# A two-layer decoder trunk on one core: a head's transposes behind the next query product, the first expert tiles' rows gathered in the router's block, blocks that end without GpSimd's drain

## What is computed

```python
for l in range(DEPTH):                       # 2 layers, 1024 tokens, D_MODEL = 1024
    h = rmsnorm(x, norm_mix[l])
    x = x + (hybrid_mixer(h, ...) if l % 2 == 0 else swa_mixer(h, ...))
    x = x + cross_attention(rmsnorm(x, norm_xattn[l]), mem_k, mem_v, w_q[l], w_o[l])
    x = x + hier_moe(rmsnorm(x, norm_ffn[l]), ...)
return rmsnorm(x, final_norm)

# hybrid_mixer, part B (4 heads; q and k are two maps of 64 each, v is 128 wide)
a = softmax(q0 @ k0.T) - lam * softmax(q1 @ k1.T)       # causal
o = rmsnorm(a @ v, subln_g) * (1 - lambda_init)         # a head's output, then the output projection
# hier_moe: 1 of 4 groups, top 2 of its 8 experts; tokens sorted by expert
xs = t[tok_sorted]; gu = ragged_dot(xs, w_gate_up, group_sizes)
y = ragged_dot(silu(gu[:, :512]) * gu[:, 512:], w_down, group_sizes) * weight
```

## Time and profile before

| | before |
|---|---|
| median of 3 runs | 2696.58 us (2696.14 to 2696.95) |
| the profiled execution's own time | 2695.93 us |
| its span | 2694.1 us |
| TensorE busy | 2460.8 us (91%) |
| VectorE, ScalarE, GpSimd busy | 858.0, 411.2, 286.7 us |
| hybrid block | 66 to 525 us |
| routers' blocks | 734 to 832 us, 1977 to 2075 us |
| experts' blocks | 833 to 1439 us, 2076 to 2649 us |

### The profile page before, as it was taken

The page is one execution under the profiler, slowest core; times in us unless marked ns, Lnnn a source line. Parts: engine busy times, 40 slices in busy tenths (PEclk is TensorE's granted clock), DMA queues, the critical chain, the costliest instruction groups (busy, mean ns, idle before and its releaser), DMA issues. The chain is left out here.

```text
span 2694.1 us, 28504 instructions
## 1 busy us (share of the span) xinstructions
PE 2460.8 (91%) x10112; PEld 1320.8 (49%) x10112; DVE 858.0 (32%) x1509; ACT 411.2 (15%) x1012; POOL 286.7 (11%) x303
## 2 busy tenths in 40 slices
PE   6999999999995999999996989989995999999992
PEld 4667676645642444444444754634552444444440
DVE  3244352653243111111114472765235111111114
ACT  2122121201210000000001150501220000000001
POOL 0000000230000000000003040341000000000003
PEclk9999999999997999999998999999997999999996
DMA  6010101105136999999996100210024899999996
GB/s 211 24 32 16 39 18 67 39 0 230 62 145 225 387 403 402 402 403 405 403 402 198 43 15 25 71 39 32 1 89 176 313 402 402 402 403 403 404 397 234
DMA packets 204306, 563.21 MB, mean 209 GB/s; under 512 B 33104, under 2 KB 70864, under 8 KB 204112
## 3 DMA queue, kind: packets, MB, share of 16 engines
q1 hardware_dynamic: 182208, 493.64, 48.3%
q0 software_dynamic: 12000, 42.74, 4.6%
q10 hardware_dynamic: 10032, 25.96, 2.5%
HBM read 506.19 MB, written 55.05 MB: 208 GB/s over the span
## 5 line engine op out<-in xcount | busy, mean ns | idle before, releaser
L2020 PE MATMUL pair<-W,yT 128*128 128x512 f32 x1056 | 465.7, 599 | 0.0
L2020 PEld LDWEIGHTS pair<-W,yT 128*128 128x128 f32 x1056 | 199.4, 191 | 241.4 <-issue 239.0
L2033 PE MATMUL pO<-hT,yT 128*64 128x512 f32 x1056 | 233.9, 595 | 12.8 <-ACT yT L2126 11.8
L2062 PE MATMUL pair<-W,yT 128*128 128x512 f32 x528 | 232.3, 593 | 0.0
L834 PE MATMUL pU<-hT,W 128*128 128x256 f32 x768 | 174.7, 380 | 5.2 <-DVE W L976 2.4
L2167 DVE TENSOR_TENSOR tmp<-probT,pair 128x512 f32<-128x512 f32 x33 | 22.7, 688 | 460.4 <-ACT probT L2105 460.4
L834 PEld LDWEIGHTS pU<-hT,W 128*128 128x128 f32 x768 | 142.2, 190 | 26.2 <-issue 5.0
L2062 PEld LDWEIGHTS pair<-W,yT 128*128 128x128 f32 x528 | 97.7, 190 | 112.1 <-issue 112.1
L2033 PEld LDWEIGHTS pO<-hT,yT 128*64 128x64 f32 x1056 | 75.4, 137 | 150.1 <-issue 150.1
L2171 DVE TENSOR_TENSOR tmp<-probT,pO 64x512 f32<-64x512 f32 x33 | 22.4, 679 | 358.8 <-ACT probT L2109 358.8
L2074 PE MATMUL pO<-yT 128*64 128x512 f32 x528 | 120.6, 598 | 1.6 <-DVE yT L2175 1.6
(11 more groups left out here) (330 smaller groups left out, 3079.0 us busy)
## 6 DMA issues: line engine op xcount, KB each, us to landing
W<-in_moe_w_gate_up_dram SPq DMA_DIRECT2D x132, 1024.0 KB, 13.1
hT<-in_moe_w_gate_up_dram SPq DMA_DIRECT2D x132, 1024.0 KB, 16.5
W<-in_moe_w_down_dram SPq DMA_DIRECT2D x66, 1024.0 KB, 16.1
yT<-in_moe_w_down_dram SPq DMA_DIRECT2D x66, 1024.0 KB, 13.6
y_rows<-prob ACTq DMA_DIRECT2D x33, 512.0 KB, 6.7
y_rows<-qk SPq DMA_DIRECT2D x31, 512.0 KB, 6.1
W<-in_hyb_w_in_dram SPq DMA_DIRECT2D x24, 512.0 KB, 3.7
y_rows<-yT ACTq DMA_DIRECT2D x66, 128.0 KB, 6.4
```

The source lines that it names most:

```text
L2020: ins = nc.tensor.matmul(A[:, 512 * h:512 * h + 512], xt_l[:, k, :], gu_l[:, k, 512 * h:512 * h + 512], start=(k == 0), stop=(k == KD - 1))
L2033: ins = nc.tensor.matmul(pO[HS * (1 - h):HS * (1 - h) + HS, :], xt_s[:, k, :], gu_s[:, k, 512 * h:512 * h + 512], start=(k == 0), stop=(k ...
L2062: ins = nc.tensor.matmul(B[:, 512 * h:512 * h + 512], ht_l[:, f, :], dn_l[:, f, 512 * h:512 * h + 512], start=(f == 0), stop=(f == 3))
```

## The change

Five edits:

1. **Head outputs.** The wait and the 8 transposes of a head's output (`turn_out`) leave the end of the loop's body and stand between the next head's Q and K products. A first, empty turn runs in the first head, and one more behind the loop. ScalarE's two copies move behind its copy of Q, VectorE's rope and the V product wait for two counts more.
2. **First rows.** VectorE writes small 128x32 tables for only two tiles (`first_oh`, `first_p`, `first_c`: the first wide and the first half tile), TensorE multiplies them with the same `slot_oh` in 32 products of its own, VectorE copies the two columns to `icol`, and GpSimd gathers the rows of both tiles in the router's block (`Routing.gpsimd`). The list of all tiles follows behind that. `experts` no longer copies and gathers the first two tiles.
3. **Weights of the tokens** are worked out while VectorE waits for the counts.
4. **Drains.** The setup, stream, Strassen, hybrid and experts blocks get `no_gpsimd_drain=True`. `end_phase` is as it was.
5. Rooms in `yT` are laid out anew, so that the gathered rows touch nothing in use.

The diff, cut to its core (the first pair of lines stands for the same edit of all five blocks; left margins are narrowed by eight):

```diff
-    with nc.Block() as block:
+    with nc.Block(no_gpsimd_drain=True) as block:
...
                     gather(c + AHEAD)
+            if rest:
+                for i in range(2):
+                    pool.wait_ge(st_done[i], 16 * (nblk // 2))
+                rest.gpsimd(pool)
...
                                            start=(b == 0), stop=(b == n))
                 ins.then_inc(weighed, 1)
...
+            def turn_out(j):
+                pe.wait_ge(sub_step, j * 4)
+                pe.wait_ge(copied1, j * 4)
+                pe.wait_ge(copied0, j * 8)
+                pe.sem_inc(passed, 1)
+                for b in range(NB):
+                    ins = nc.tensor.transpose(C[:, b * P:(b + 1) * P], ofull[:, b, :], ident[:])
+                    if b % 4 == 3:
+                        ins.then_inc(o_turned, 1)
             with pe.Fori(1, 5) as j:
                 pe.wait_ge(exped, j * 16)
                 project(j, W_Q, A)
+                turn_out(j)
                 project(j, W_K, B)
-                pe.wait_ge(o_stored, j * 2)
+                pe.wait_ge(o_stored, j * 2 + 2)
                 pe.wait_ge(raw_done, j * 2 + 1)
...
                         project_chunk(j, chunk_at(n) + i)
-                pe.wait_ge(sub_step, j * 4 + 4)
-                pe.wait_ge(copied1, j * 4 + 4)
-                pe.wait_ge(copied0, j * 8 + 8)
-                for b in range(NB):
-                    ins = nc.tensor.transpose(C[:, b * P:(b + 1) * P], ofull[:, b, :], ident[:])
-                    if b % 4 == 3:
-                        ins.then_inc(o_turned, 1)
+            turn_out(5)
...
                 act.wait_ge(gated, j * 4)
                 nc.scalar.activation(raw[:, :], A, ACT.Copy, scale=0.125).then_inc(raw_done, 1)
+                for h in range(2):
+                    act.wait_ge(o_turned, j * 2 + h + 1)
+                    nc.scalar.activation(
+                        yT[:, bass.ds(j + 2, 1), 512 * h:512 * h + 512].rearrange("p a n -> p (a n)"),
+                        C[:, 512 * h:512 * h + 512], ACT.Copy, scale=subln[:, 0:1]).then_inc(o_stored, 1)
...
                         c_chunk(j, chunk_at(n) + i)
-                for h in range(2):
-                    act.wait_ge(o_turned, j * 2 + h + 1)
-                    nc.scalar.activation(
-                        yT[:, bass.ds(j + 3, 1), 512 * h:512 * h + 512].rearrange("p a n -> p (a n)"),
-                        C[:, 512 * h:512 * h + 512], ACT.Copy, scale=subln[:, 0:1]).then_inc(o_stored, 1)
+            for h in range(2):
+                act.wait_ge(o_turned, 5 * 2 + h + 1)
+                nc.scalar.activation(yT[:, 7, 512 * h:512 * h + 512], C[:, 512 * h:512 * h + 512],
+                                     ACT.Copy, scale=subln[:, 0:1]).then_inc(o_stored, 1)
...
                     at = j * 8 + 4 * t
                     dve.wait_ge(raw_done, j * 2 + t + 1)
-                    dve.wait_ge(o_turned, j * 2)
+                    dve.wait_ge(o_turned, j * 2 + 2)
...
+    def gpsimd(self, pool):
+        l = self.l
+        pool.wait_ge(self.first_kept, 1)
+        gather_rows(pool, xg_l, icol[:, 0:1], rows_l_loaded[l])
+        gather_rows(pool, xg_s, icol[0:HS, 1:2], rows_s_loaded[l])
...
                                    ident[:, 0:SLOTS], start=True, stop=True)
         ins.then_inc(self.item_rows, 1)
         for i in range(2 * NB):
             if i % NB == 0:
                 pe.wait_ge(self.slot_sides, i // NB + 1)
+            for side in (self.first_p, self.first_c):
+                ins = nc.tensor.matmul(self.first_ps, self.slot_oh[:, i, :], side[:, i, :],
+                                       start=(i == 0 and side is self.first_p),
+                                       stop=(i == 2 * NB - 1 and side is self.first_c))
+        ins.then_inc(self.first_listed, 1)
+        pe.wait_ge(self.tile_sides, 1)
+        for i in range(2 * NB):
             for side in (self.tile_p, self.tile_c):
                 ins = nc.tensor.matmul(self.list_ps, self.slot_oh[:, i, :], side[:, i, :],
                                        start=(i == 0 and side is self.tile_p),
...
         then(nc.vector.tensor_tensor(pe2, top[:, 1, :], top[:, 0, :], ALU.subtract))
         dve.sem_inc(self.pair_exp, 1)
+        dve.wait_ge(self.group_exp, 3)
+        then(nc.vector.tensor_reduce(gsum, gexp, AX, ALU.add))
+        dve.wait_ge(self.pair_exp, 2)
+        then(nc.vector.tensor_scalar(w1, pe2, 1.0, None, ALU.add))
+        then(nc.vector.tensor_tensor(w1, w1, gsum, ALU.mult))
+        then(nc.vector.reciprocal(wgt[:, 0, :], w1))
+        nc.vector.tensor_tensor(wgt[:, 1, :], wgt[:, 0, :], pe2, ALU.mult)
         dve.wait_ge(self.ranked, 1)
...
         then(nc.vector.tensor_tensor(rem, posf, t128, ALU.subtract))
         dve.wait_ge(cleared, 16 * len(unwritten))
-        then(nc.vector.tensor_tensor(self.tile_oh, bc(t128, NTT),
-                                     starts.unsqueeze(1).broadcast_to([P, NP, NTT]), ALU.is_equal))
-        nc.vector.tensor_scalar(self.tile_p, self.tile_oh, pidx, None, ALU.mult)
-        nc.vector.tensor_tensor(self.tile_c, self.tile_oh, bc(blk, NTT), ALU.mult)
+        then(nc.vector.tensor_tensor(
+            self.first_oh, bc(t128, 2),
+            starts.rearrange("p (a b) -> p a b", a=2)[:, :, 0].unsqueeze(1).broadcast_to([P, NP, 2]),
+            ALU.is_equal))
+        nc.vector.tensor_scalar(self.first_p, self.first_oh, pidx, None, ALU.mult)
+        nc.vector.tensor_tensor(self.first_c, self.first_oh, bc(blk, 2), ALU.mult)
         for i in range(2):
             b = slice(NB * i, NB * i + NB)
             nc.vector.tensor_tensor(self.slot_oh[:, b, :], iota_bc(NB, TS), bc(rem[:, b], TS),
                                     ALU.is_equal).then_inc(self.slot_sides, 1)
-        dve.wait_ge(self.group_exp, 3)
-        dve.wait_ge(self.pair_exp, 2)
-        then(nc.vector.tensor_reduce(gsum, gexp, AX, ALU.add))
-        then(nc.vector.tensor_scalar(w1, pe2, 1.0, None, ALU.add))
-        then(nc.vector.tensor_tensor(w1, w1, gsum, ALU.mult))
-        then(nc.vector.reciprocal(wgt[:, 0, :], w1))
-        nc.vector.tensor_tensor(wgt[:, 1, :], wgt[:, 0, :], pe2, ALU.mult)
         then(nc.vector.tensor_scalar(shift, t128, 0.5, -0.5 * SLOTS * TS, ALU.mult, ALU.add))
         then(nc.vector.tensor_scalar(shift, shift, 0.0, None, ALU.max))
         nc.vector.tensor_tensor(pos_u[:, :, :].rearrange("p i c -> p (i c)"), posf, shift, ALU.subtract)
+        dve.wait_ge(self.first_listed, 1)
+        nc.vector.tensor_copy(icol[:, :], self.first_ps).then_inc(self.first_kept, 1)
+        then(nc.vector.tensor_tensor(self.tile_oh, bc(t128, NTT),
+                                     starts.unsqueeze(1).broadcast_to([P, NP, NTT]), ALU.is_equal))
+        nc.vector.tensor_scalar(self.tile_p, self.tile_oh, pidx, None, ALU.mult)
+        nc.vector.tensor_tensor(self.tile_c, self.tile_oh, bc(blk, NTT), ALU.mult).then_inc(self.tile_sides, 1)
         dve.wait_ge(self.listed, 1)
         nc.vector.tensor_copy(slots[0:TS, :], self.list_ps)
...
+def gather_rows(pool, dst, index, loaded):
+    pool.indirect_dma_start(dst, None, h_dram, bass.IndirectOffsetOnAxis(ap=index, axis=0)).then_inc(loaded, 16)
...
                 pool.wait_ge(idx_s, count)
                 pool.sem_inc(passed, 1)
-                pool.indirect_dma_start(xg_s, None, h_dram,
-                                        bass.IndirectOffsetOnAxis(ap=icol[0:HS, 1:2], axis=0)
-                                        ).then_inc(got_s, 16)
-            gather_l(0, 1)
-            gather_s(SLOTS, 1)
+                gather_rows(pool, xg_s, icol[0:HS, 1:2], got_s)
             with pool.Fori(1, rounds(pool)) as i:
                 pool.wait_ge(xl_turned, i * 2)
-                gather_l(i, i + 1)
+                gather_l(i, i)
                 pool.wait_ge(xs_turned, i)
-                gather_s(i + SLOTS, i + 1)
+                gather_s(i + SLOTS, i)
```

More of the change, by code:

```diff
@@ L1879, in build @@
         dnl_loaded = [[sem(f"moe{l}_wide_down_loaded{c}", keep=True) for c in range(2)] for l in range(2)]
+        rows_l_loaded = [sem(f"moe{l}_wide_rows", keep=True) for l in range(2)]
+        rows_s_loaded = [sem(f"moe{l}_half_rows", keep=True) for l in range(2)]
+        xg_l, xg_s = yflat[:, 0:1024], prob[0:HS, 0:1024]
+        def gather_rows(pool, dst, index, loaded):
+            pool.indirect_dma_start(dst, None, h_dram, bass.IndirectOffsetOnAxis(ap=index, axis=0)).then_inc(loaded, 16)
         def gate_up_rows(l, e, c):
@@ L1913, in experts @@
             passed = sem(n_ + "_passed")
-            xg_l, xg_s = yflat[:, 0:1024], prob[0:HS, 0:1024]
             xt_l = yflat[:, 1024:2048].rearrange("p (k n) -> p k n", k=KD)
```

15 lines of the change are left out of this document (10 added, 5 removed).

## The result

The changed kernel takes **2680.99 us** (median of 5 runs, 2680.87 to 2682.71) beside 2696.14 for the kernel before (5 runs): 15.2 us less, ratio 0.9946 with a 95% interval of 0.9931 to 0.9961. The profiled executions show 13.4 us of it: spans of 2694.1 and 2680.7 us (the changed kernel's profiled run, 2682.71, is its slowest).

What follows compares the result with a forecast made beforehand. TensorE, busy 9 of 10 in most slices, was taken as the bound, so only its waits count: -5.0 us hybrid and -3.0 us experts' starts make -8.0, 2688.6 us against 2696.58; range 2682.5 to 2694.5.

Steps and rivals of the forecast that it cites:

- the removed drain is paid at the next one: Router blocks' ends: the wait for gathers moves to the drains at L90 and L92, ending 1.4 us past the landing.
- rival A: Drains at L90 and L92 don't wait for gathers; TensorE starts at the first landing: -12.3, 2684.3 us; chance 0.18.
- Rival C: Drain behind a gather costs 8.4 us from its own start, at L90 and L92: +14.9, 2711.5 us; chance 0.04.
- the 8.4 us row: End of the experts' blocks: a GpSimd drain lasting 8.4 us, 1.4 past the last gather's landing, cited against short drains.
- The hybrid block, -5.0: Heads' ends: TensorE's wait goes in three heads of four, -5.9 us, one empty set of transposes adds 0.9; net -5.0.
- 3 x 1.96: Hybrid block: TensorE's wait at a head's end removed in three heads of four, 5.9 us.
- rival D: Hybrid block gives nothing: the turn holds up rope or V, the 1.96 us come back; 2694.5 us; chance 0.08.
- the cover: Hybrid block: a rope 1 us late is hidden, TensorE being in the V product until 216.25, then two chunks.
- Elsewhere I cost the edit at nothing: Block ends other than the routers': leaving out GpSimd's drains changes nothing, 0 us.
- The router's part: Router's block ends 2.9 us later, but early gathers start the experts 1.0 and 2.0 us earlier: -3.0 in all.
- Rival B: Gathers land only with the end of the weights' burst: +2.7 per layer, 2697.0 us, no change; chance 0.08.
- Behind that start nothing changes: Experts' blocks: after TensorE's earlier start, transposes, first products and loads keep their distances; no further gain or loss.

Runs made afterwards that it cites:

- experiments 3 and 4: 3: kernel before with first rows gathered in the router's block, drains kept, 2694.59 us; 4: changed kernel with drains back in both router blocks, 2686.86 us.
- Experiment 2: Kernel before with only the heads' turns moved behind the query product: 2691.50 us, ratio 0.9979.
- experiment 1: Kernel before with GpSimd's drain left out of all twelve block ends, nothing else: 2697.19 us, ratio 0.9999.
- experiment 9: Kernel before with the first rows gathered in the router's block and no drains, heads' turns where they were: 2689.64 us, ratio 0.9973.
- experiment 6: Changed kernel with SyncE's 6 MB of expert weights issued in the experts' block, behind the gathers: 2675.07 us, ratio 0.9920.
- experiment 5: Changed kernel run again, nothing altered, beside the kernel before: 2680.39 us, ratio 0.9941.
- experiment 14: Kernel before run once more, unaltered, for a second profiled execution: 2699.73 us, one execution.
- experiment 8: Changed kernel with the 6 MB of weights issued behind the gathers and 26 unused transposes keeping TensorE busy ahead of the experts: 2675.67 us, ratio 0.9921.

## Why the prediction was wrong

- **The step that failed: "the removed drain is paid at the next one".** It isn't. L90 and L92 take 0.10 and 0.04 us with two gathers in flight. Only the drain that stands at a block's own end waits for them, until 0.1 to 0.2 us behind the second landing (experiments 3 and 4), and that is the one which the change leaves out. That was rival A, given 0.18. Its marks, shifted by the lead that the changed kernel has at the tables in the profile (8.19 and 8.65 us), are 830.0 and 2074.2 us for the transposes, measured 830.64 and 2072.65; its total was 2684.3. Rival C, a drain of fixed length, falls with the same traces: there was none to pay at L90 and L92, and where it is paid it lasts 10.4 to 11.2 us, as the landing does. The sentence in the prediction that spoke against rival A, that the trace calls all of these drains the same instruction, was too weak for the weight it got: a name doesn't tell what an instruction waits for. The Trainium skill's Perfetto Trace Analysis, section "DMA Instruction — SWDGE (GPSIMD)", puts the profiler's end of such an instruction where its descriptors are written; the trace agrees, with instructions of 1.25 and 1.10 us and landings of 8.7 and 9.0. The prediction took it for a sign of short drains, and set that aside by the 8.4 us row. The page says nothing on drains either way: a drain behind the same instructions takes 0.10 us at L90 and 11.2 at the block's own end.
- **The hybrid block, -5.0: right in kind, mis-sized as "3 x 1.96".** The wait went as said, and the empty turn cost 0.87 (forecast 0.9). With the wait went 0.24 us more at each switch, which is 2.20 a boundary, and behind these waits the falls of the clock, 1.67 us each, one or two in each of the seven executions. In the two profiles: 6.6 + 1.67 - 0.87 = 7.4 us, against 5.0. Experiment 2's own total, -5.7 by its ratio, has an interval of -8.1 to -3.2. The clock had no term in the sum at all, and no reason was given for that. The rope's shuffle starts 15.3 us behind Q (15.2 forecast): rival D is out. One reading beside it was wrong without harm: the row of the V product in the earlier trace rows is cut at the window's edge, and the product runs for 14.46 us and not 7.31, so that the cover is larger than counted.
- **"Elsewhere I cost the edit at nothing"**: right, experiment 1.
- **The router's part:** block's end 1.9 us later behind its tables (2.9 forecast), gather issued 4.56 us behind them (5.1), landings 8.77 and 8.23 us (7.6 and 9.1 in rival A). From the tables to the first transposes the profiles give 3.0 us in the first layer and 5.1 in the second, forecast 1.0 and 2.0. By experiment 9 the part gave -7.3 us and not -3.0. Rival B is out: in the changed kernel the rows land at 830.64 and 2072.65, and the fifth of the six loads only at 832.6 and 2075.3. But its cause was real: the burst delays the rows by 3.2 us, which experiment 6 takes back. The Trainium skill, in DMA: Bandwidth & Descriptors, "Queues, rings and completion order", says that each engine takes turns between its queues; the 5.56, 6.71 and 8.77 us with 0, 4 and 6 MB ahead in layer 0, and rows that land ahead of loads issued before them, agree.
- **"Behind that start nothing changes":** not in each execution. Of 11.21 us at the first transposes of layer 0, 8.3 were left at the block's end, as the clock was low for longer (16.82 us for the first 32 products, 15.51 before) and fell again at 854 us. In experiment 5 the second fall isn't there, and the kernel before has it in experiment 14.
- Together: 7.4 for the hybrid (from the profiles) and 7.3 for the rows (from experiment 9's ratio) make 14.7 of the 15.2 and 15.8 us of the two comparisons; with experiment 2's own 5.7 it is 13.0. The intervals hold both sums, and don't fix the split between the parts to better than some 2.5 us. The range ended at 2682.5 with A's fastest landings, and left no room for a hybrid part above 5.0.

## What to carry to other kernels

In these runs GpSimd's drain at a block's end cost nothing that shows as long as no gather was in flight ahead of an engine that needed the end (experiment 1), and lasted until the landing once two were: an edit that starts transfers ahead of a block's end and one that removes the drain must be judged as one (0.9987 and 0.9999 apart, 0.9973 together; in the trace 6.2 us at the first transposes). Ask of each wait at a boundary what it has been seen to wait for, one by one; a name shared in the trace is no evidence. Small transfers that release an engine should be issued ahead of bulk loads which nobody needs yet: moving 6 MB from 8 us ahead of the gather to 6 us behind it gave 5 us.

## What the runs showed that was not expected

TensorE's granted clock can fall from 2.4 to 1.2 GHz behind an idleness of only 2 us, for three to four microseconds of the work that follows. Of three like boundaries in one loop it did so at the second in six executions of seven, at the third in four, and at the first never. One fall costs 1.7 us here, nearly as much as the wait itself: taking away a wait of 1.96 us was worth 2.2 us, and 3.9 where a fall went with it. In the experts the falls at 854 us (changed kernel) and at 2089 us (experiment 8) stand behind two waits in a row, of 1.41 and some 0.5 us. They come in six of 32 places, with and without the change, in one execution of a kernel and not in the next; what decides it there, and why the first boundary never has one, wasn't tried. A difference of one or two microseconds between two profiled executions is no finding until these windows have been compared.
